# Position mixing behind the last B gate and in wider products, the first merge gate ahead of the keys, and the rotary angles earlier on VectorE

## The reference

```python
# A: per group g of 128 channels, mixing over the 128 positions of a block
mask = pos_chunk[None, :] <= pos_chunk[:, None]          # chunks of 64
w = jnp.where(mask[None], w_s, 0)
mixed = jnp.einsum('gts,bnsgc->bntgc', w, layer_norm(v)) + b_s...
# B: four pooled groups, each with a gate
y_b = (multiscale_pool(b_x, pool_w, pool_scale) * silu(b_z)) @ w_b_out
# C: latent attention; queries and keys turned by rotary angles
ang = positions[:, :, None] * freqs;  cos, sin = jnp.cos(ang), jnp.sin(ang)
q = rms_norm(c_q, cq_g) @ w_uq;  kv = rms_norm(c_kv, ckv_g) @ w_ukv
# merge: a sigmoid gate for each branch and channel
merged = sum(sigmoid(gates_k) * y_k for k in (A, B, C, D))
```

## Time and profile before

| | |
|---|---|
| median of 3 runs | 1366.23 us (1366.23 to 1366.48) |
| the profiled execution | 1367.47 us, of which its span is 1365.6 us |
| TensorE matmuls busy | 1355.8 us, 99% of the span |
| VectorE, ScalarE, GpSimd busy | 695.9, 560.9 and 606.1 us |
| mean granted TensorE clock | 0.997 of full |

### The profile page before, as it was taken

One profiled execution on the slowest core, in us unless ns is written; L12 is line 12 of the kernel. 1 busy time (PEld: TensorE's weight loads), 2 busy tenths in 40 slices (PEclk: granted clock), 3 DMA queues, 4 the chain that ended last, 5 costly groups with the idle time before them and its releaser, 6 DMA issues.

```text
span 1365.6 us, 16177 instructions
## 1 busy us (share of the span) xinstructions
PE 1355.8 (99%) x6417; PEld 1140.0 (83%) x6417; DVE 695.9 (51%) x1063; ACT 560.9 (41%) x870; POOL 606.1 (44%) x455
## 2 busy tenths in 40 slices
PE   9998999999999999999999999999999999999998
PEld 8887888888888888888888888888888888888887
DVE  7896454144453333264778965451545432243743
ACT  6355463255552222224444554443555422222242
POOL 2544242544335544445464542424433444544543
PEclk9999999999999999999999999999999999999999
DMA  7221222322223333323243222223222233333332
GB/s 206 93 85 62 78 93 62 93 87 83 78 78 101 100 93 96 121 93 93 93 116 94 84 80 76 78 63 97 89 78 77 93 93 96 105 93 108 102 99 94
DMA packets 68269, 126.32 MB, mean 92 GB/s; under 512 B 9041, under 2 KB 37985, under 8 KB 68193
## 3 DMA queue, kind: packets, MB, share of 16 engines
q1 hardware_dynamic: 66960, 124.72, 29.4%
q10 hardware_dynamic: 1232, 0.55, 0.1%
HBM read 123.15 MB, written 2.10 MB: 92 GB/s over the span
## 4 chain that ended last, share of the span: by engine, by line
PE 93%; DVE 5%; ACT 1%; DMA 1%; issue 0%; POOL 0%; SPq 0%; DVEq 0%
PE ps L490 30%; PE ps L492 29%; PE ps L491 29%; PE ps L769 1%; PE ps L704 1%; PE ps L805 1%; PE ps L691 1%; DVE n_t L1451 1%; DVE h_lo L1338 0%; PE ps L535 0%; DVE trail_a L1486 0%; DMA x<-x_in 0%; PE ps L550 0%; PE ps L545 0%; DVE vn_lo L1338 0%
## 5 line engine op out<-in xcount | busy, mean ns | idle before, releaser
L463 POOL TENSOR_TENSOR w_lo<-w_raw,w_hi 128x512 fp32r<-128x512 f32 x222 | 304.3, 1371 | 735.2 <-ACT w_hi L977 735.1
L490 PE MATMUL ps<-h_hi,w_hi 128*128 128x512 f32 (+1 forms) x1160 | 453.6, 391 | 3.7 <-DVE mix_off L1575 3.7
L492 PE MATMUL ps<-h_hi,w_lo 128*128 128x512 f32 (+1 forms) x1160 | 451.0, 389 | 0.0
L491 PE MATMUL ps<-h_lo,w_hi 128*128 128x512 f32 (+1 forms) x1160 | 450.9, 389 | 0.0
L977 ACT ACTIVATE w_hi<-w_raw 128x1024 fp32r<-128x1024 f32 x227 | 238.5, 1053 | 174.1 <-PE ps L492 169.3
L465 POOL TENSOR_TENSOR w_lo<-w_raw,w_hi 128x512 fp32r<-128x512 f32 x222 | 304.9, 1373 | 0.0
L490 PEld LDWEIGHTS ps<-h_hi,w_hi 128*128 128x128 f32 x1160 | 218.5, 188 | 49.1 <-DVE mix_off L1575 3.9
L492 PEld LDWEIGHTS ps<-h_hi,w_lo 128*128 128x128 f32 x1160 | 218.4, 188 | 45.2
L491 PEld LDWEIGHTS ps<-h_lo,w_hi 128*128 128x128 f32 x1160 | 218.5, 188 | 43.6
L1774 DVE SCALAR_TENSOR_TENSOR m_part<-th,ps 128x512 f32<-128x512 f32 x48 | 33.0, 687 | 237.9 <-PE ps L492 237.7
L1203 ACT ACTIVATE th<-ps 128x512 f32<-128x512 f32 x48 | 28.7, 597 | 183.5 <-PE ps L492 183.5
(11 more groups left out here) (330 smaller groups left out, 1992.8 us busy)
## 6 DMA issues: line engine op xcount, KB each, us to landing
w_raw<-w_in SPq DMA_DIRECT2D x180, 512.0 KB, 3.5
w_raw<-w_in SPq DMA_DIRECT2D x92, 128.0 KB, 2.4
w_raw<-w_in SPq DMA_DIRECT2D x36, 256.0 KB, 3.0
x<-x_in SPq DMA_DIRECT2D x8, 256.0 KB, 5.1
w_raw<-w_in SPq DMA_DIRECT2D x32, 64.0 KB, 2.1
out_x<-x SPq DMA_DIRECT2D x7, 256.0 KB, 4.0
p_raw<-p_in SPq DMA_DIRECT2D x2, 512.0 KB, 5.1
w_raw<-w_in ACTq DMA_DIRECT2D x4, 128.0 KB, 3.0
```

The lines of the kernel that those rows point to most:

```text
L463: pool.tensor_tensor(w_lo_t[s][:, 0:4, :], w_raw_t[s][:, 0:4, :], w_hi_t[s][:, 0:4, :].bitcast(F32), ALU.subtract)
L490: pe.matmul(o, a_hi, b_hi, start=first, stop=False, skip_group_check=skip)
L491: pe.matmul(o, a_hi, b_lo, start=False, stop=False, skip_group_check=skip)
L492: return pe.matmul(o, a_lo, b_hi, start=False, stop=last, skip_group_check=skip)
```

## The change

1. `mix` goes behind `bz3` in the order of the chunks and in the queues. The sums of its weights go to bank 6, once B's second group is out of it.
2. The high and low parts of the mixing weights now stand in one tile. `vn_hi` is multiplied by both at once, 256 columns wide, into two columns' worth of PSUM (two banks a group, `MIX_BANKS`); `vn_lo` by the high part, 128 columns. DVE adds the two halves: two dependent instructions a group instead of one.
3. The third mixing group waits for `off_made`, the fourth for the first `mix_taken`.
4. `gb0` goes ahead of `kq0` in TensorE's queue and in the order of the chunks, into bank 5.
5. The rotary angles go ahead of the scaling of x by the norms on DVE, and the transpose of the frequencies that they need goes into the middle of `av1` on TensorE. `rope_tables` goes behind all of `mix_t`.
6. The banks of the latents and of B's gates are dealt anew.

```diff
-    names += ["bz0", "vp", "bz1", "bz2", "mix", "bz3"]
+    names += ["bz0", "vp", "bz1", "bz2", "bz3", "mix"]
...
-        names += [f"kq{p}", f"gb{d}", f"yb{2 * p}", ...
+        names += [f"gb{d}", f"kq{p}"] if p == 0 else [f"kq{p}", f"gb{d}"]
...
-BZ_BANKS, K_BANK, POOL_BANKS = (7, 4, 6, 5), (6, 4), (1, 0, 6, 5)
+BZ_BANKS, K_BANK, GATE_BANK, TURN_BANK, POOL_BANKS = (7, 6, 5, 4), (6, 4), (5, 6), (4, 7), (1, 0, 4, 5)
+LAT_BANKS, MIX_BANKS = (6, 4, 5), (0, 2, 6, 0)
...  TensorE, front
-                for g in range(G):
-                    if g < 2:
-                        pe.wait_ge(pooled, after(l * G + 3 - g))
+                for g in range(G):
+                    if g == 2:
+                        pe.wait_ge(off_made, after(l))
+                    if g == 3:
+                        pe.wait_ge(mix_taken, after(l * G))
                     for t in range(TB):
-                        last = mm3(ps[:, g * 512 + t * P:g * 512 + (t + 1) * P], vn_hi[:, t, g * P:(g + 1) * P],
-                                   vn_lo[:, t, g * P:(g + 1) * P], w_hi[:, g, :], w_lo[:, g, :])
-                pe.wait_ge(off_made, after(l))
-                project(l, "bz3", 5)
+                        o, v = MIX_BANKS[g] * 512 + t * 2 * P, slice(g * P, (g + 1) * P)
+                        pe.matmul(ps[:, o:o + 2 * P], vn_hi[:, t, v], w_both[:, g::G, :], start=t % 2 == 0, stop=False,
+                                  skip_group_check=True)
+                        last = pe.matmul(ps[:, o:o + P], vn_lo[:, t, v], w_both[:, g, :], start=False, stop=True,
+                                         skip_group_check=True)
...  TensorE, pair_c
                 if p == 0:
-                    pe.wait_ge(act_b_made, after(l * G + 2))
+                    gate_b(l, d, gate, act_b_made, l * G + 2)
+                    pe.wait_ge(mix_taken, after(l * G + 3))
+                chunk(l, f"kq{p}")
...
                 if p == 0:
-                    gate_b(l, d, fill, mix_taken, l * G + 3)
-                    branch_b(l, d, fill + 1, act_b_made, l * G + 3)
+                    branch_b(l, d, turn, act_b_made, l * G + 3)
...  ScalarE, pair_c
+                first = kq if p else f"gb{d}"
+                if p == 0:
+                    gate_b(l, d, fill)
...
                 last.then_inc(q_taken, 1)
-                weights_up_to(l, kq, 3)
+                weights_up_to(l, first, 3)
...  VectorE, front
+                def mix_taken_out(g):
+                    settle(dve.scalar_tensor_tensor(to, both[:, :, 1, :], sm("ln_col", g),
+                                                    over(mix_off[:, g, :], [P, TB, P], 1), ALU.mult, ALU.add))
+                    dve.scalar_tensor_tensor(to, both[:, :, 0, :], sm("ln_col", g), to, ALU.mult, ALU.add).then_inc(
+                        mix_taken, 1)
...
+                mix_taken_out(0)
                 gate_z(3)
                 gate_p(3)
+                mix_taken_out(1)
                 b_low(3)
+                mix_taken_out(2)
+                mix_taken_out(3)
+                rope_tables()
```

More of the change, by code:

```diff
@@ L449, in _ @@
                     c = number(l, name)
-                    s, n = c % RING, width(name)
+                    s = c % RING
                     if 0 < c < RING:
@@ L508, in project_rows @@
                     k = 2 * i + u
+                    if rope_frequencies and u:
+                        pe.wait_ge(freq_made, after(0))
+                        pe.wait_ge(lat_taken, after(0))
+                        pe.transpose(ps[:, FREQ_AT:FREQ_AT + P], freq_b[:], ident[:]).then_inc(freq_ready, 1)
                     if name.startswith("lat"):
@@ L569, in rope_rows @@
                 pe.wait_ge(gain_diag, after(l))
+                if l == 0:
+                    pe.wait_ge(freq_taken, after(0))
                 pe.wait_ge(rows_loaded, (l + 1) * 32)
@@ L719, in pair_c @@
                 d, head, n, lp = 4 * p, PAIR * p, l * G + PAIR * p, l * 2 + p
-                w_hi, w_lo = chunk(l, f"kq{p}")
+                w_hi, w_lo = w_hi_t[number(l, f"kq{p}") % RING], w_lo_t[number(l, f"kq{p}") % RING]
                 q_hi = w_hi[:].rearrange("p k c -> p (k c)")
@@ L732, in pair_c @@
                 for t in range(TB):
-                    if p == 0:
-                        pe.wait_ge(mix_taken, after(l * G + t))
-                    else:
+                    if p:
                         if t == 0:
@@ L760, in pair_c @@
                                           lambda t: q_tok[:, t, 1, :])):
-                    if p == 0 and b == 4:
+                    if p == 0 and b == gate:
                         pe.wait_ge(gb_tanh, after(l * KD + d + 1))
-                    if p == 0 and b == 5:
+                    if p == 0 and b == turn:
                         pe.wait_ge(yb_taken, after(l * KD + d + 1))
@@ L1052, in latents_high @@
                     act.wait_ge(lat_ready, after(l * 3 + u))
-                    act.activation(o, bank(4 + u), ACT.Copy, scale=gain).then_inc(lat_hi_made, 1)
+                    act.activation(o, bank(LAT_BANKS[u]), ACT.Copy, scale=gain).then_inc(lat_hi_made, 1)
                 copied(3)
@@ L1086, in front @@
                                    ACT.Copy).then_inc(v_hi_made, 1)
-                bz(1, 4)
-                weights_up_to(l, "mix")
+                bz(1, BZ_BANKS[1])
+                weights_up_to(l, "bz3")
                 for g in reversed(range(G)):
@@ L1102, in front @@
                 b_high(1)
-                bz(2, 6)
-                weights_up_to(l, "kq0")
+                weights_up_to(l, "mix")
+                bz(2, BZ_BANKS[2])
+                weights_up_to(l, "gb0")
                 b_high(2)
@@ L1109, in front @@
                     act.activation(cs_tok[:, :, 1, :], ang[:], ACT.Sin).then_inc(rope_sines, 1)
-                act.wait_ge(*end_of(l, "mix"))
-                weights_up_to(l, "gb0")
-                bz(3, 5)
+                bz(3, BZ_BANKS[3])
+                weights_up_to(l, "kq0")
                 b_high(3)
@@ L1187, in pair_c @@
                 keys_high(n + 1, 1)
-                weights_up_to(l, kq, 10)
+                weights_up_to(l, first, 10)
                 gate_c(l, head + 1, 1)
-                weights_up_to(l, kq, 11)
+                weights_up_to(l, first, 11)
                 out_high(n + 1, head + 1, 7)
@@ L1574, in front @@
                     c = slice(g * P, (g + 1) * P)
-                    last = dve.scalar_tensor_tensor(mix_off[:, g, :], bank(5)[:, c], sm("ln_col", G + g), rows[:, c],
+                    last = dve.scalar_tensor_tensor(mix_off[:, g, :], bank(6)[:, c], sm("ln_col", G + g), rows[:, c],
                                                     ALU.mult, ALU.add)
@@ L1578, in front @@
                 dve.wait_ge(off_made, after(l))
-                rope_tables()
-                for g in range(G):
+                if l == 0:
+                    dve.wait_ge(rope_sines, after(0))
+                def mix_taken_out(g):
                     if g < G - 1:
@@ L1584, in front @@
                         dve.wait_ge(*end_of(l, "mix"))
[L1585 to L1588, removed]
+                    o = MIX_BANKS[g] * 512
+                    both = ps[:, o:o + 8 * P].rearrange("p (t u s) -> p t u s", t=TB, u=2)
+                    to = mix_t[:, g, :].rearrange("p (t s) -> p t s", t=TB)
+                    settle(dve.scalar_tensor_tensor(to, both[:, :, 1, :], sm("ln_col", g),
[3 more added lines that the diff above has]
+                mix_taken_out(0)
                 gate_z(3)
                 gate_p(3)
+                mix_taken_out(1)
                 b_low(3)
+                mix_taken_out(2)
+                mix_taken_out(3)
+                rope_tables()
             def branch_b(l, d, b):
```

82 lines of the change are left out of this document (42 added, 40 removed).

## The result

The changed kernel runs in 1371.05 us (median of 7 runs, 1369.49 to 1372.19) against 1366.23 us before (7 runs, 1365.76 to 1367.54). The ratio is 1.0032, with a 95% interval of 1.0022 to 1.0043. It is slower by 4.8 us, where 3.5 were forecast. The profiled execution took 1371.05 us for a span of 1369.3 us, at a mean granted clock of 0.995 (before: 1365.6 us and 0.997).

What follows compares the result with a forecast made beforehand. TensorE, busy 99% of the span, was taken to bound the kernel, so only its stream and few waits count. −6.34 − 3.2 + 0.5 + 8.56 + 4.0 = +3.5 us on 1366.23 gives 1369.7 us, range 1366.3 to 1372.0.

Steps and rivals of the forecast that it cites:

- The wait that goes: Layer 0, ahead of `bz3`: TensorE's wait for DVE's `mix_off` vanishes, 3.87 us directly and 2.47 by the clock, −6.34 us.
- The angles in their new place: DVE ahead of the scaling of x: the angles take about 3.3 us, hidden in idle time, so cost nothing.
- The narrower mixing and its small waits: Mixing in both layers: a block falls from 0.332 to 0.231 us, saving 3.2 us; new small waits cost 0.5.
- the prediction's signs: Listed for the profile after: among them, mixing without sums lasting 3.7 to 3.9 us, with 0.12 and 0.11 between starts.
- the zero-slack place of the prediction: Last `mix_t` ahead of `kq0`: DVE done at 9.4 us, TensorE there at 9.4; DVE late had chance 0.08.
- The wait that comes: Ahead of `gb1`, each layer: weights converted late behind `q_sq` and `q_tok` on ACT; TensorE stands 4.28 us, 8.56 together.
- The clock behind it: Behind the new waits ahead of `gb1`: the lower clock level costs 2.0 us each, 4.0 together.
- The sum: Whole kernel: −6.34 − 3.2 + 0.5 + 8.56 + 4.0 = +3.5 us, giving 1369.7 us.
- the old wait: TensorE's wait for `mix_off` in layer 0 of the kernel before, ahead of `bz3`: 3.87 us and 2.47 by the clock.

Runs made afterwards that it cites:

- the first experiment: The changed kernel with ACT converting `gb1`'s weights right behind the squares of the keys, ahead of its wait for the end of `kq0`: 1358.16 us.
- the 2.73 us case: The changed kernel with `gb1`'s conversion on ACT moved between the squares and the copies of the queries: 1365.13 us.
- `gb1` early and narrow products: The changed kernel with `gb1`'s weights converted ahead of ACT's wait for `kq0`'s end, and each 256-column mixing product split into two of 128: 1360.39 us.

## Why the prediction was right

**The wait that goes.** Forecast −6.34 us, and −6.0 by the angles alone in the kernel before. The cause was the angles, as the prediction had it. The prediction gave two reasons, that `bz3` now stands ahead of the sums and that the angles have left their place, and only the second takes the wait away: with the angles in the old place `bz3` waits for nothing, but the mixing itself waits 3.06 us.

**The angles in their new place.** Costed at nothing, rightly. The timeline of DVE in the changed kernel has their first operation, their last, and the scaling of x:

```profile
35.96 0.67 DVE L1394 CAST pos_f<-pos_i 128x4 f32<-128x4 int32 x1
...
39.08 0.23 DVE L1403 TENSOR_SCALAR turns<-turns 128x128 f32<-128x128 f32 x1
40.00 3.10 DVE L1476 SCALAR_TENSOR_TENSOR n_t<-x,par,r_b 128x512 f32<-128x512 f32 x2 [0.70 <-ACT r_b L1044]
```

They take 39.31 − 35.96 = 3.35 us here (3.3 forecast, 5.67 in the old place), and 0.70 us of cover is left. The estimate was near, but one comparison behind it was not sound: the first operation has 4 elements a partition and the last 128 (see the forms in the earlier trace rows and here), not as few. The sound one is the last operation against itself, 1.18 us there and 0.23 here.

**The narrower mixing and its small waits.** Forecast −3.2 and +0.5, together −2.7; measured −2.2 by the medians. The block of 0.231 us was right, though its two starts stand 0.17 and 0.06 us apart and not 0.12 and 0.11, as the prediction's signs had it. The mixing without its sums lasts 4.00 us, for 3.7 to 3.9 forecast, as the wait at the fourth group is 0.37 us with the slow product behind it, for 0.2 or 0.25. The weighing of row against page was right too. The isolated distance of the Trainium skill, "TensorE: Matmul & The Clock Gate", "Back-to-back issue gap", would have had the two forms equal. The same section says that this distance counts too little for short products in a stream, where it gives about 81 ns for 128 columns; this trace has 111 and agrees with neither figure. The end of the last `mix_t` was the zero-slack place of the prediction; it left about 0.3 us:

```profile
109.93 0.75 DVE L1611 SCALAR_TENSOR_TENSOR mix_t<-ps,small,mix_t 128x512 f32<-128x512 f32 x1
```

It ends at 110.68, and `kq0` starts at 110.97, when `gb0` is through.

**The wait that comes.** Forecast 4.28 us a layer, measured 4.27. That it was the place in ACT's queue, and nothing else, is shown by the first experiment.

**The clock behind it.** Forecast 2.0 each; in the profiled execution it was 7.95 − 5.48 = 2.47 and 2.49, and 4.4 for both by the medians. This is the term that was mis-sized, low by 0.4 to 1.0 us. The prediction shaved the one row it had, 2.47, to 2.0 because a fall that comes later would cost less. The runs show the contrary, a later fall costs more: 1.65 us where the clock read 0.71 over a wait of 5.91, 2.5 where it read 0.87 over an equal one, and 3.3 where it held 1.00 to the end of a wait of 3.06. In the two new waits it read 0.81 and 0.82, near the 0.78 of the old one, and the price was that of the old one as well. That the clock would fall at all rested on a single row; the 2.73 us case shows that such a fall is not certain.

**The sum** with what was measured: −6.0 − 2.2 + 12.9 = +4.7 us, and the result is +4.8. That these agree is in good part arithmetic, since the three differences nearly form one chain of kernels. What the chain tests is its one open joint: the kernel before with the angles moved (1360.60) and the changed kernel with `gb1` early and narrow products (1360.39) are alike, so nothing else in the change moved the time. The forecast of +3.5 lay 1.3 short, with rounding: 0.3 by the old wait, 0.5 by the mixing, 0.4 by the clock; the three misses had one sign, and none hid another. The place of a single line in ACT's queue costs 12.9 us, more than all the gains.

## What to carry to other kernels

When a step is moved that was covering a wait, list every chain that runs beside it in its old place, not only the one that it will cover in the new. Here `gb0` covered the conversion of the next weights, and that conversion stood behind work that depends on the step before it. Put the conversion of weights ahead of the first instruction in its queue that waits for the current product; it needs only the raw data and a free slot. And on an engine that is 99% busy, find the few waits first: moving ten small VectorE operations into an idle stretch was worth 6 us, the regrouping of products 2.

## What the runs showed of the hardware

- **Waits of TensorE and its clock.** Two waits of 1.25 us cost only themselves. One of 2.73 us brought the lower clock (1.2 GHz) once and left it at 2.4 GHz once in the same execution. One of 3.06 us kept 1.00 to its end, and the level fell as work resumed; it cost 3.3 us by the clock in that execution and 2.6 by the medians. One of 3.87 us cost 2.47. Two waits of 4.27 us cost 4.4 together by the medians, two of 5.1 us 4.1, and two of 5.91 us 3.9. The later in a wait the level fell, the more it cost: 1.65 and 2.5 us behind the two of 5.91. What decides when it falls is not settled here; the length of the wait alone does not.
- **Small VectorE operations beside GpSimd.** The same ten operations took 5.67 us in the old place and 3.35 in the new one. Six of them took the same in both, and the first less in the old place (0.16 against 0.67 us; GpSimd stood still there, and here it was at work until 36.60). The other three ran 1.18 to 1.27 us there, with GpSimd at work from 98.06 on, and 0.23 to 0.29 in the new place, where GpSimd stood still by then, until 39.57. The gate of B that followed at 102.02, which reads and writes PSUM, took its usual 0.68 us with GpSimd at work.
